# Order of the first stages in a hybrid encoder layer: one FFN1 turn ahead of the memory's keys and values

## The reference

```python
def rmsnorm(x, g):
    y = x * lax.rsqrt(jnp.mean(x * x, axis=-1, keepdims=True) + EPS)
    return y * g

def swiglu_ffn(x, g, w_gate, w_up, w_down):
    h = rmsnorm(x, g)
    return (jax.nn.silu(h @ w_gate) * (h @ w_up)) @ w_down

def memory_kv(mem, g, wk, wv):
    m = rmsnorm(mem, g)
    return m @ wk, m @ wv            # (256, 1024) each

x = x + 0.5 * swiglu_ffn(x, ffn1_norm, ffn1_w_gate, ffn1_w_up, ffn1_w_down)   # D_FF = 2816
# ... token mixers, cross attention over memory_kv(mem_prompt), a second FFN, final norm
```

## Time and profile before

| what | us |
|---|---|
| median of 3 runs | 3371.97 |
| the profiled execution, first to last instruction | 3372.3 |
| TensorE busy | 3238.2 (96%) |
| VectorE busy | 1322.0 (39%) |
| GpSimd busy | 957.6 (28%) |
| ScalarE busy | 679.5 (20%) |

### The profile page before, as it was taken

One profiled execution on the slowest core, in us unless ns is written; L12 is line 12 of the kernel. 1 busy time (PEld: TensorE's weight loads), 2 busy tenths in 40 slices (PEclk: granted clock), 3 DMA queues, 4 the chain that ended last, 5 costly groups with the idle time before them and its releaser, 6 DMA issues.

```text
span 3372.3 us, 50147 instructions
## 1 busy us (share of the span) xinstructions
PE 3238.2 (96%) x19977; PEld 3078.3 (91%) x19977; DVE 1322.0 (39%) x2297; ACT 679.5 (20%) x1326; POOL 957.6 (28%) x436
## 2 busy tenths in 40 slices
PE   6899999999999999989999999999899999999998
PEld 5899999999978888888987989988799999999997
DVE  3233233233356555653342456242325332333324
ACT  5100000000033333433433242133311000000001
POOL 3533433333322222211012034222133333333341
PEclk9999999999999999999999999999999999999999
DMA  5411111111141233212111145024311111111111
GB/s 193 136 41 37 44 49 38 44 44 43 42 163 64 106 129 136 76 41 70 58 50 68 53 157 176 26 97 160 127 38 45 44 43 44 44 37 43 37 44 63
DMA packets 93338, 248.70 MB, mean 74 GB/s; under 512 B 11664, under 2 KB 50320, under 8 KB 90512
## 3 DMA queue, kind: packets, MB, share of 16 engines
q1 hardware_dynamic: 48640, 154.09, 13.9%
q10 hardware_dynamic: 44560, 92.60, 7.6%
HBM read 197.87 MB, written 48.79 MB: 73 GB/s over the span
## 4 chain that ended last, share of the span: by engine, by line
PE 87%; DVE 6%; issue 3%; ACT 2%; POOL 1%; DMA 1%; ACTq 1%; DVEq 0%; POOLq 0%
PE psum L164 60%; PE psum L260 12%; PE psum L1797 1%; DVE n_tmp L557 1%; PE psum L1733 1%; PE psum L939 1%; PE psum L2765 1%; PE psum L1009 1%; POOL w_lo L2272 1%; PE psum L984 1%; PE psum L2738 1%; DVE a_sc L1334 1%; PE psum L1747 1%; PE psum L1741 1%; PE psum L2744 1%
## 5 line engine op out<-in xcount | busy, mean ns | idle before, releaser
L131 POOL TENSOR_TENSOR w_hi<-w_raw,zero 128x1024 fp32r<-128x1024 f32 x199 | 383.2, 1926 | 2108.2 <-PE psum L164 1318.5
L164 PE MATMUL psum<-x_hi,w_hi 128*128 128x384 f32 x2928 | 575.8, 336 | 18.6 <-issue 4.6
L164 PE MATMUL psum<-x_lo,w_hi 128*128 128x384 f32 x2928 | 572.4, 335 | 0.0
L164 PE MATMUL psum<-x_hi,w_lo 128*128 128x384 f32 x2928 | 569.8, 334 | 0.0
L164 PEld LDWEIGHTS psum<-x_hi,w_hi 128*128 128x128 f32 x2928 | 513.4, 188 | 27.8 <-issue 13.9
L164 PEld LDWEIGHTS psum<-x_lo,w_hi 128*128 128x128 f32 x2928 | 514.2, 188 | 1.9
L164 PEld LDWEIGHTS psum<-x_hi,w_lo 128*128 128x128 f32 x2928 | 513.1, 188 | 0.0
L134 POOL TENSOR_TENSOR w_lo<-w_raw,w_hi 128x1024 fp32r<-128x1024 f32 x199 | 494.3, 2484 | 15.6
L419 DVE TENSOR_TENSOR f_hid<-psum,f_gate 128x384 f32<-128x384 f32 x132 | 73.6, 557 | 860.6 <-PE psum L164 858.2
L366 ACT ACTIVATE f_gate<-psum 128x384 f32<-128x384 f32 x132 | 64.8, 493 | 1479.8 <-PE psum L164 1476.1
L164 PE MATMUL psum<-f_h_hi,w_hi 128*128 128x384 f32 x1056 | 269.5, 336 | 0.0
(11 more groups left out here) (303 smaller groups left out, 3380.3 us busy)
## 6 DMA issues: line engine op xcount, KB each, us to landing
w_raw<-units SPq DMA_DIRECT2D x224, 512.0 KB, 3.6
gate_dram<-b_stash ACTq DMA_DIRECT2D x48, 192.0 KB, 1.9
e_gate<-gate_dram ACTq DMA_DIRECT2D x48, 192.0 KB, 2.6
a_kc<-k_cache ACTq DMA_DIRECT2D x4, 2048.0 KB, 7.6
a_vc<-v_cache ACTq DMA_DIRECT2D x4, 2048.0 KB, 12.7
proj_dram<-a_cv ACTq DMA_DIRECT2D x12, 576.0 KB, 2.8
b_pad<-proj_dram SPq DMA_DIRECT2D x12, 576.0 KB, 4.8
x_sk<-mem_k ACTq DMA_DIRECT2D x6, 1024.0 KB, 7.8
```

What stands on the lines that cost most here:

```text
L131: pool.tensor_tensor(k.w_hi[s][:, :], k.w_raw[s][:, :], k.zero[:, 0:1].to_broadcast([P, D]), ALU.add)\
L164: mm = pe.matmul(out, wl if part == 2 else wh, (xl if part == 1 else xh)[:, n0:n1], start=(part == 0 and i == 0), stop=(part == 2 and i == ...
```

## The change

FFN1's first turn becomes a stage of its own, `begin`, ahead of `memory`; `ffn1` keeps ten turns. The tokens come in three transfers, the first third first of all; the other two and the memory are issued among FFN1's first units (class `Start`). The norm n1 is done in `begin`: its first two thirds ahead of the first product, the last third within the turn, which now goes by thirds. Squares are shared: ScalarE takes one half, VectorE the other half of the first third, GpSimd the other half of the second, ScalarE both of the last. The memory's own norm is the `tail` of `begin`, under the down products. In the memory stage no norm is left, and its unit 0 is split ahead by GpSimd (`split_next`), as is FFN1's next unit at its end. Some buffers have new addresses, and `host_unit` picks the units of the first three stages in the new order from the same array.

```diff
-def split_units(pool, k, turns, jobs, first=None, left=None):
+def split_units(pool, k, turns, jobs, first=None, left=None, then=None):
...
     for j in range(turn):
         if j or not k.split_ahead:
             one(0, j)
+        if then and j == 0:
+            then()
...
+def split_next(pool, k, turns, turn, done):
+
+    pool.wait_ge(k.dense_done.sem, k.dense_done.at(done))
+    pool.wait_ge(k.raw_landed[0].sem, k.raw_landed[0].at(16 * len(sharing(0, turn)) * turns + 16))
+    pool.tensor_tensor(k.w_hi[0][:, :], k.w_raw[0][:, :], k.zero[:, 0:1].to_broadcast([P, D]), ALU.add)\
+        .then_inc(k.unit_hi.sem, 1)
...
     def sync(sp):
-        load_units(sp, k, k.next_unit, turns, 6)
+        if start:
+            load_units(sp, k, k.next_unit, turns, 6, lambda i: start.load_x(sp, 1), lambda: start.load_rest(sp))
+        else:
+            load_units(sp, k, k.next_unit, turns, 6)
...
+        if start:
+            start.scalar(act)
+            turn(0, gates_of(0)[0:1])
+            norm.upper(act, 1)
+            start.wait_x(act, 2)
+            norm.square(act, 2)
+            turn(0, gates_of(0)[1:2])
+            norm.gather(act, 2)
+            norm.root(act, 2)
+            turn(0, gates_of(0)[2:3])
+            norm.upper(act, 2)
+            turn(0, gates_of(0)[3:])
+            start.scalar_behind(act, tail)
+            return
...
+                    if start:
+                        if n == 1:
+                            tail.scale_chunk(dve, 0, d)
+                        if n == 2 and d == 2:
+                            tail.lower_both(dve, 0)
+                        continue
...
+    def load_rest(self, sp):
+
+        self.load_x(sp, 2)
+        sp.dma_start(self.mem[:], by_frame(self.k.memt)).then_inc(self.k.x_loaded.sem, 16)
...
+    def square_other(self, eng, n):
+
+        s = self.norm.s
+        self.wait_x(eng, n)
+        if n:
+            eng.wait_ge(s.nsq.sem, s.nsq.at(2 * n))
+        self.norm.square_other(eng, n, 1)
+
+    def tensor(self, pe):
+        self.norm.sums(pe, 0, True)
+        self.norm.total(pe, 0)
+        self.norm.sums(pe, 1, True)
+
+    def scalar(self, act):
+        act.preload_act_table_set("natural_log_exp_and_others")
+        self.wait_x(act, 0)
+        self.norm.square(act, 0, (0,))
+        self.norm.gather(act, 0)
+        self.norm.root(act, 0)
+        self.wait_x(act, 1)
+        self.norm.square(act, 1, (0,))
+        self.norm.upper(act, 0)
+        self.norm.gather(act, 1)
+        self.norm.root(act, 1)
+
+    def scalar_behind(self, act, own):
+
+        k = self.k
+        for sig in self.norm.s.nsplit:
+            act.wait_ge(sig.sem, sig.at(self.norm.nb))
+        act.wait_ge(k.x_loaded.sem, k.x_loaded.at(16))
+        act.preload_act_table_set("natural_log_exp_and_others")
+        own.square(act, 0)
+        own.gather(act, 0)
+        own.root(act, 0)
+        own.upper(act, 0)
+
+    def vector(self, dve):
+        k = self.k
+        self.square_other(dve, 0)
+        dve.wait_ge(k.loaded.sem, k.loaded.at(0))
+        for n in range(2):
+            self.norm.scale(dve, n)
+            self.norm.lower_both(dve, n)
...
-    pe_norm = {3: [lambda pe: norm.sums(pe, 0)], 5: [lambda pe: norm.total(pe, 0), lambda pe: norm.sums(pe, 1)],
-               7: [lambda pe: norm.total(pe, 1), lambda pe: norm.sums(pe, 2)], 9: [lambda pe: norm.total(pe, 2)]}
...
-        own_norm.scalar(act)
-        act.wait_ge(k.x_loaded.sem, k.x_loaded.at(16))
-        for j in range(2):
-            unit_upper(j)
+        act.wait_ge(k.unit_split.sem, k.unit_split.at(1))
+        unit_upper(1)
...
-                for dst, src in ((mem[:], by_frame(k.memt)), (k.gains[:], k.gains_dram), (k.ident[:], k.ident_dram)):
+                sp.dma_start(x_early[:, :, 0:THIRD], by_frame(k.xt)[:, :, 0:THIRD]).then_inc(k.x_landed[0].sem, 16)
+                for dst, src in ((k.gains[:], k.gains_dram), (k.ident[:], k.ident_dram)):
                     sp.dma_start(dst, src).then_inc(k.loaded.sem, 16)
-                sp.dma_start(x_early[:], by_frame(k.xt)).then_inc(k.x_loaded.sem, 16)
-                sp.wait_ge(k.loaded.sem, k.loaded.at(48))
...
-        run_stages(nc, memory, ffn1, attention, delta, merge, mix, cross,
+        run_stages(nc, begin, memory, ffn1, attention, delta, merge, mix, cross,
                    wo, ffn2, last)
```

More of the change, by code:

```diff
@@ L195, in enter @@
         k.ahead = min(RING, k.turn_sizes[self.phase]) if 0 < self.phase < len(k.turn_sizes) else 0
[L196 removed]
+        k.split_ahead = self.phase > 0
         return self
@@ L270, in finished, with ffn_phase @@
         return [3 * self.main + g for g in range(self.count) if a < (g + 1) * self.PIECES <= b]
-def ffn_phase(nc, k, name, norm, x, xh, xl, work, tail, bias_rows=None, memory=None):
-    turns = NFF // 2
+def ffn_phase(nc, k, name, norm, x, xh, xl, work, tail, bias_rows=None, memory=None, turns=NFF // 2, start=None):
     h_hi = nc.alloc_sbuf_tensor_at(name + "_h_hi", [P, 2, T], F32R, offset=work)
@@ L284, in ffn_phase @@
     LAST = turns - 1
+    SUMMED, TOTAL = ({2: 2}, {0: 1, 3: 2}) if start else ({1: 2}, {2: 2})
     def order_of(i):
@@ L323, in turn @@
                 mm = product(pe, k.ps[g % NPS][:, 0:THIRD], tiles, n * THIRD, (n + 1) * THIRD,
-                             (lambda: norm.total(pe, 2)) if order is by_third and g == 2 else None)
+                             (lambda: norm.total(pe, TOTAL[g])) if order is by_third and g in TOTAL else None)
                 mm.then_inc(k.dense_done.sem, 1)
-                if order is by_third and g == 1:
-                    norm.sums(pe, 2)
+                if order is by_third and g in SUMMED:
+                    norm.sums(pe, SUMMED[g])
                 if memory and isinstance(i, int) and i == 0 and g == 0:
@@ L345, in turn @@
                     g += 1
+                    if start:
+                        if n == 0 and d == 4:
+                            tail.sums(pe, 0)
+                        if n == 1 and d == 0:
+                            tail.total(pe, 0)
+                        continue
                     if isinstance(i, int) and i == LAST and n >= 1 and d == 4:
@@ L349, in turn @@
                         tail.total(pe, n - 1)
-        if memory:
-            memory.norm_split(pe)
+        if start:
+            start.tensor(pe)
         turn(0)
-        with pe.Fori(1, LAST) as i:
-            turn(i)
-        turn(LAST)
+        if LAST:
+            with pe.Fori(1, LAST) as i:
+                turn(i)
+            turn(LAST)
     def scalar(act):
@@ L440, in turn @@
                             tail.lower_both(dve, 0)
-        if norm:
+        if start:
+            start.vector(dve)
+            hidden(0, 0, 1)
+            norm.scale(dve, 2)
+            norm.lower_both(dve, 2)
+        elif norm:
             norm.scale(dve, 2)
@@ L457, in ffn_phase @@
         norm.done()
+    if start:
+        start.done()
+        tail.done()
     k.dense_done.base += JOBS * turns
@@ L505, in square, with square_other, sums @@
                 .then_inc(s.nsq.sem, 1)
-    def sums(self, pe, n):
+    def square_other(self, eng, n, h):
+        c = slice(4 * h, 4 * h + 4)
+        x = self.x[:, c, self.cols(n)]
+        eng.tensor_tensor(self.squares[:, c, self.square_cols(n)], x, x, ALU.mult).then_inc(self.s.nsq.sem, 1)
+    def sums(self, pe, n, both=False):
         k, s = self.k, self.s
+        if both:
+            pe.wait_ge(s.nsq.sem, s.nsq.at(2 * n + 2))
         for c in range(KD):
-            if c % 4 == 0:
+            if c % 4 == 0 and not both:
                 pe.wait_ge(s.nsq.sem, s.nsq.at(2 * n + c // 4 + 1))
@@ L2247, in stored, with memory_phase @@
             act.wait_ge(sig.sem, sig.at(32))
-def memory_phase(nc, k, own_norm, norm, xh, xl, work, end):
+def memory_phase(nc, k, own_norm, xh, xl, end):
     kv, nat = end.kv, end.nat
-    pe_norm = {3: [lambda pe: norm.sums(pe, 0)], 5: [lambda pe: norm.total(pe, 0), lambda pe: norm.sums(pe, 1)],
-               7: [lambda pe: norm.total(pe, 1), lambda pe: norm.sums(pe, 2)], 9: [lambda pe: norm.total(pe, 2)]}
[L2256 to L2260, removed]
     UNITS = 2 * KD
@@ L2295, in tensor @@
                 turn(j - 1)
-            for step in pe_norm.get(j, []):
-                step(pe)
     def scalar(act):
@@ L2327, in scalar, with vector @@
                 act.dma_start(k.mem_turned[j - 1], nat[:, (j - 1) % 2, :]).then_inc(k.kv_slot[(j - 1) % 2].sem, 16)
[L2328 to L2334 removed]
+    def vector(_):
+        pass
     stage = Stage(k, sync, gpsimd, tensor, scalar, vector)
[L2337 to L2338 removed]
     units_done(k, 1, UNITS)
[L2340 removed]
     n = UNITS
```

113 lines of the change are left out of this document (61 added, 52 removed).

## The result

The changed kernel takes 3378.0 us in the median (3368.3 to 3384.3, 20 runs), the kernel before 3373.3 us beside it (3365.2 to 3379.9, 20 runs). The ratio is 1.0016, with a 95% interval of 1.0009 to 1.0022: 0.16% slower, inside the 0.2% that I called no change. The forecast was 3359.1 us and the range ended at 3376.

A forecast was written before the change was run, and what follows sets the result against it. TensorE, busy for 96% of the span, bounds the kernel. Head 32.4, first turn 81.8, memory stage 54.6 and second turn 79.4 sum to 248.2 for 261.09 us: gain 12.9, forecast 3359.1 us, range 3348 to 3376.

The forecast's parts named there:

- The head: Start up to the first product: with POOL's work blocking DVE's scalings, it comes at 32.4 us, 9.1 us later than before.
- rival A: Head: no contention between DVE and POOL, so the head costs nothing more; 3350 us, chance 0.15.
- FFN1's first turn: FFN1's first turn with the norm's remaining parts in it: 81.8 us, bounds 78 and 87.
- rival B: FFN1's first turn: the last third is late, TensorE waits 3 to 6 us at the seventh product; 3364 us, chance 0.15.
- The memory norm under the down products: End of FFN1's first turn: the memory's norm fits under 24 down products and costs nothing; 2 us if cover fails.
- The memory stage: Stage of the memory's keys and values, freed of the norm: 54.6 us in place of 83.5.
- about every third store behind a load: Memory stage: every third store lands late behind a weight load, mostly hidden under two products ahead; 3.3 us a gap.
- the twelve gaps: Mid-memory-stage intervals between product starts, taken at 3.3 us each, bounds 3.15 and 5.31.
- rival C: Memory stage: every turned store lands late behind a weight load, gaps take 5.3 us; +24 us, 3383 us, chance 0.15.
- Nothing after 261 us differs: After two FFN1 turns and the memory stage: any difference past 261 us would make the prediction wrong.
- the list of what else moves: Rest of the kernel: FFN1 keeps ten old-form turns, bias-row excess of 4.5 us stays, SP's extra transfers are hidden.
- Same: Whole kernel: a time within about 0.2% (6.7 us), not distinguishable from no change; chance 0.17.

The follow-up runs named there:

- headfree: Changed kernel with POOL kept still while VectorE makes the first third, its square of the second third given to ScalarE: 3368.3 us, ratio 0.9989.
- after_again: Changed kernel run once more, unchanged, for the spread of its parts between executions: 3379.3 us, ratio 1.0015.
- before108: Kernel before with 216 fulfilled waits (108 instructions) on TensorE, giving its later loop heads the changed kernel's places in the fetch blocks: 3381.5 us, ratio 1.0024.
- buf4: Changed kernel with four buffers in place of two for the memory's keys and values and their turned copies: 3360.1 us, ratio 0.9958.
- buf4pad: Changed kernel with four memory-stage buffers in place of two and 48 padding instructions on TensorE: 3346.6 us, ratio 0.9924.
- pad148: Changed kernel with 296 fulfilled waits (148 instructions) on TensorE, so loop heads have their places in the block as in the kernel before: 3374.4 us, ratio 1.0003.
- pad48: Changed kernel with 96 fulfilled waits (48 instructions) on TensorE, moving every later loop 48 instructions on: 3365.4 us, ratio 0.9974.
- headpad: Changed kernel with POOL kept still during the first third and 48 padding instructions on TensorE, two buffers as before: 3353.2 us, ratio 0.9945.
- best: Changed kernel with all three edits: POOL kept still during the first third, four memory-stage buffers, 48 padding instructions: 3341.7 us, ratio 0.9913.

## Why the prediction was right and wrong

**The head: right.** 31.46 us for 32.4. The chain held at each step: the first third had landed for the squares at 7.6 us (7.4), VectorE's first scaling began at 15.08 (15.5) and ended at 16.7, 0.4 us after POOL's square, where I had it blocked until 17.2. The last three came after POOL's unit 2, and x_lo ran free at 3.42 us. What I overrated was POOL's square, 2.75 us for 3.7, and the total, 0.94 us for 1.65. headfree confirms the cause and rival A's price (23 us).

**FFN1's first turn: right.** 82.05 us for 81.8. There was no gap ahead of the seventh product; rival B didn't happen. The memory norm under the down products cost nothing. That the sum fits to 0.3 us is in part luck: from 31.46 to 40 us the granted clock is 0.69, which by an estimate is 5.3 us at the lower level and a loss of 2.6 us where I took 1.8, so the sums, totals and waits cost about 4.5 where I took 5.1.

**The memory stage: the mechanism right, its size wrong.** The step that failed is "about every third store behind a load, and most of that hides under the two products that are ahead. I take 3.3". In the trace 12 of the copies waited for the turned store, and the twelve gaps were 3.72 us (120.44 to 165.09) in after, 4.08 in after_again and 4.31 in headfree. That is between my value and rival C's 5.3, just under the 4.4 at which I said that it decides. The twelve gaps were mis-sized by 5.0 us in the first trace and the stage by 6.2, in the mean of the seven traces by some 10. In my walk through the order a late store delayed one unit. In the chip's order it also delays ACT's upper half of the next unit, so POOL's half and the next load: TensorE waited for m_kv five times and for w_lo six.

**Nothing after 261 us differs: wrong.** I had named a difference there as what would make the prediction wrong. The step that failed is the list of what else moves: the change makes TensorE's program longer, and I priced that at nothing without naming it. It put the attention loop's head near the end of a fetch block, so that each return to the head waits for two blocks one after the other, the second in the middle of a product: 6.8 us in the first trace, 3.5 in the second, and 8.2 in before108, where it stands alone.

**The sum.** Forecast 3359.1, less 0.9 for the head, plus 0.3 for the first turn, plus 9.9 for the memory stage (64.5 for 54.6), plus 5.1 for the loop's starts (mean of 6.8 and 3.5): 3373.5 us, where 3378.0 was measured. Of the 4.5 us left, 1.3 are the level that I started from: before's median was 3372.0 in the three runs I had and 3373.3 in the twenty. The rest is not settled. After's traces have other differences of their own behind 930 us, of 1 to 6 us each, which come and go between executions. The largest is TensorE's wait for b_vb in the delta loop, 3.91 us at 1727 us: 2.5 to 4.1 us in all traces with the change but those of buf4 and buf4pad, 1.28 in before108, 1.03 in before. With the slower matmuls behind it, it takes 5.7 us, but by 1879 us 4.7 of them are back, which before's own trace loses and, in part, only pad148's besides. I can't say that the change has no part in these.

**The chances.** "Same" had 0.17. C as I priced it (3383) didn't come; some 10 of its 24 us and a loss that no rival had came together. With pad148, where the loops lie as before, the change with its memory stage of 65 us is worth nothing (1.0003); with pad48 0.26%; with the wait and the contention removed as well 0.87%. Two versions of before that this comparison asks for were not run. One has four buffers: there ACT's copies waited 4.8 us in all for those stores, so it isn't shown what they would give without the change. The other has pad48's placing, which by the table would be worth some 3.4 us to before too (an estimate); that much of the 0.87% isn't owed to the change.

## What to carry to other kernels

When a change adds or removes instructions ahead of a loop, write down by how many its head moves on each engine, modulo the fetch block, and over how many blocks a turn is then spread; read the duration of the loop's branch and the packets of the instruction queue in the trace, and expect microseconds either way at each return to the head of a long loop; compare two versions at equal placing, or at each one's best, before judging the edit. When a stage is freed of the work that held it, price the next wait from several executions and ask for a buffer instead of an estimate: two more buffers turned waits of up to 4.7 us into none. And give contention between two engines an experiment that keeps one still for the short critical stretch; here two lines gave 8 us at the first product.

## What the runs showed of the hardware

TensorE can stop between two matmuls of one accumulation for 1.7 to 3.3 us with no wait in the code. The place moves with the program: 8 instructions more ahead of the loop moved it by four matmuls, from after the seventh to after the third, and 256 bring the old picture back. Behind ten of the twelve such stalls in six traces the next eight matmuls took 2.3 to 2.8 us for 1.55, on the lower clock; there a start costs 3.2 to 5.7 us against before's. Behind the two of after_again, the longer of which was 2.53 us, they took 1.56, and the starts cost 1.2 and 2.3.

The Trainium skill (Runtime: NRT & Kernel Launch, Instruction fetch mechanics) names the branch to a target outside the window as the stall, and the trace agrees: this loop's branch back takes 3.3 to 4.2 us where its target is fetched, and 0.2 us where no packet is fetched (pad48, buf4pad, headpad, best). The skill also calls the crossing of a block mostly hidden. Where the next block begins seven or three matmuls behind such a branch, it wasn't: it cost the 1.7 to 3.3 us above in twelve of twelve cases. FFN1's shorter loop, 905 instructions a turn, had branches of 0.2 to 0.3 us in before and in after, with no packet of the instruction queue from 322 to 861 us in after.

A placing with which the attention loop isn't fetched anew (pad48) made its starts free, 1.6 to 1.8 us better each than in the kernel before.
